# Adding the first four weighted V rows to the residual on VectorE, in a fused two-layer transformer kernel

## The chip, the cores and the metric

The kernel runs on one core of one Trainium2 chip. The metric is the device time of one execution in microseconds; lower is better. Engines are called TensorE (PE in the rows, with PEld for its weight loads), VectorE (DVE), ScalarE (ACT), GpSimd (POOL) and SyncE (SP, which only issues transfers here).

## The reference, cut to what matters

The kernel computes two whole layers on 256 tokens of width 1024 in float32. The part that the change touches is the second half of the first layer, a retrieval feed-forward: each token has 8 heads, each head picks 16 of 16,384 experts, and each expert is a row of U (for the dot product with the token) and a row of V (that is added with a weight).

```python
def peer_ffn(xn, w_q, sub_keys, u, v):
    q = (xb @ w_q).reshape(PEER_BLOCK, PEER_HEADS, 2, PEER_HALF)
    s = jnp.einsum('thpd,hpnd->thpn', q, sub_keys)      # scores of the sub-keys
    ...                                                  # top 16 of each head: expert, best
    g = jax.nn.softmax(best, axis=-1)
    act = jax.nn.gelu(jnp.einsum('td,thkd->thk', xb, u[expert]), approximate=False)
    return jnp.einsum('thk,thkd->td', (g * act).astype(xb.dtype), v[expert])
...
h = h + peer_ffn(hn, ...)
```

A token has 8 x 16 = 128 picks ("slots"). Tokens lie on the 128 partitions, in two tiles (n = 0 and 1), so the stage handles 2 x 128 = 256 "rows". Row k is, for every token of tile k // 128, the 2048 floats (U and V side by side) of its expert in slot k % 128: 1 MB gathered from memory.

## The kernel before, in words

The stages ahead of this one (first norm, projections, gated linear attention, output projection) end near 180 us of the trace, and the second layer begins near 860 us. Between them lies the retrieval stage. Its work, by engine:

- **SyncE** loads the eight pieces of the query weights (L684, each 1 MB, into five homes in turn), then waits for `v_done` of the batch that holds the first row in home `mixT` (row 6, so batch 3, L685), loads a 1 MB piece of the second layer's memory weights there (L687), and two more into query homes 0 and 1 (L690) once query groups 5 and 6 are done (L689).
- **TensorE** runs, for i = 0 to 7, `query_features(i)` (L1899: 16 float32 products of 128x256, which the trace shows as 32 passes), then `key_scores` of the group before (L2120). In i = 4, 5 and 6 it also runs two batches of `weighted_rows` (L2123 to L2131), so batches 0 to 5 stand between the query groups; the others follow in the loop at L2145. A batch is two rows. `weighted_rows(b)` waits for `diag_done`, and multiplies diag(weight of the row) by the V half of the row (two products of 128x512 per row, four passes in the trace, L2129), summed in two PSUM banks per tile of tokens over all 128 rows. It ends with `v_done` + 1.
- **VectorE** finds the picks of a head (`search_head`: some 40 small instructions, L1437 to L1502) and takes the dot product of the token with the U half of each row (`dot_rows`, L1548). It works in program order: search_head(0), search_head(1), rows 0 to 3, softmax(0), rows 4 to 7, search_head(2), rows 8 to 15, then head by head in the same pattern. At the end of a tile `add_peer` (L1516) adds the PSUM sums to `resid`.
- **ScalarE** copies query groups and key scores out of PSUM (`out_query`, L904; `out_scores`, L987) and runs `weigh(b)` for each batch: GELU of the dots (L1011, waits for `dot_done`), times the softmax weight (L1014, waits for `soft_done`), and the diagonal matrices (L1019), for which there are four buffers. In its order weigh(0) and weigh(1) follow out_scores(2); weigh(2) and weigh(3) follow out_scores(3); weigh(4) and weigh(5) follow out_query(5) and out_scores(4); weigh(6) and weigh(7) follow out_query(6) and out_scores(5). `out_scores(i)` waits for key_scores(i), which TensorE runs behind query_features(i + 1).
- **GpSimd** issues the gathers in order of rows (L805), each into a "home" of 8 KB per partition. A row in a home used before waits until the batch of the earlier row is summed (L800, `v_done`).

Homes near the change: rows 0 to 3 lie in early0 to early3, row 4 in ring5, 5 in query1, 6 in mixT, 7 in ring3 (free when query group 3 is done), 8 in ring4 (query group 4). Rows 9, 10, 11 and 12 reuse the homes of rows 0, 1, 2 and 3; rows 13, 14, 15 and 16 those of rows 4, 5, 7 and 8; rows 17, 18 and 19 those of 9, 10 and 11. Row 20 is the first in ring2, which is free when **query group 7**, the last one, is done (`home_ready`, L782). Row 21 (actT) waits for the same, rows 22 and 23 for the last key scores. As the issues are in order, no row behind row 20 can start before it.

```python
            for i in range(PH):
                query_features(i)
                ...
                elif i > 2:
                    key_scores(i - 1)
                if 4 <= i < PH - 1:
                    weighted_rows(2 * i - 8)
                    weighted_rows(2 * i - 7)
            key_scores(PH - 1)
            for b in range(2 * PH - 10, BATCHES):
                weighted_rows(b)
```

Of the kernel before, what the change touches and what calls it, by code (L numbers as in the profile page):

```python
# [9 lines left out]
ALU = mybir.AluOpType  # L10
# [4 lines left out]
D = 1024  # L15
# [18 lines left out]
PH = 8  # L34
HP = 2 * PH
NKEY = 128
TOP = 16
SLOTS = PH * TOP
# [2 lines left out]
PICKS = 2 * TOP  # L41
BATCH = 2
ROWS = NT * SLOTS
BATCH_ENDS = [*range(BATCH, ROWS - BATCH + 1, BATCH), ROWS - 1, ROWS]
BATCHES = len(BATCH_ENDS)
BATCHES_0 = SLOTS // BATCH
DIAGS = 2 * BATCH
# [39 lines left out]
def batch_of(k):  # L87

    return next(b for b, end in enumerate(BATCH_ENDS) if k < end)


def rows_of(b):

    return range(BATCH_ENDS[b - 1] if b else 0, BATCH_ENDS[b])

# [21 lines left out]
def build(nc, t, out):  # L117
    ctx = ExitStack()
    with ctx:
# [3 lines left out]
        def sem(name):  # L123
            return ctx.enter_context(nc.semaphore(name))
# [92 lines left out]
        mixT = take1(KC, T)  # L217
# [57 lines left out]
        soft_exp = sem("soft_exp")  # L275
        soft_done = sem("soft_done")
        dot_done = sem("dot_done")
        diag_done = sem("diag_done")
        v_done = sem("v_done")
        hq0a_then_mkv_moved = sem("hq0a_then_mkv_moved")  # L280
        peer_out = sem("peer_out")
# [135 lines left out]
        def row_count(k):  # L417

            return 16 * (rows_in[home_of[k]].index(k) + 1)

        def home_free(name):

            return batch_of(rows_in[name][-1]) + 1

        def unit_of(u):

# [222 lines left out]
        def _(sp):  # L649
# [28 lines left out]
            for i in range(PH):  # L678
# [3 lines left out]
                    sp.wait_ge(*query_used(i - WQ_HOMES))  # L682
                src = t["peer_w_q"][:, i * T:(i + 1) * T].rearrange("(c p) n -> p c n", p=P)
                sp.dma_start(wq_view(i), src).then_inc(wq_loaded[i % WQ_HOMES], 16)  # L684
            sp.wait_ge(v_done, batch_of(rows_in["mixT"][0]) + 1)  # L685
            sp.wait_ge(cols_then_mem_loaded, 80)
            sp.dma_start(mixT, w_mem[:, :, T:2 * T]).then_inc(cols_then_mem_loaded, 16)  # L687
            for k in range(2):
# [38 lines left out]
        def _(pool):  # L727
# [62 lines left out]

            for k in range(ROWS):
                n, s = k // SLOTS, k % SLOTS
                if k == PICKS * (UNITS - 2):
                    inverse_rms(0)
                if k % TOP == 0:
                    pool.wait_ge(idx_done, k // TOP + 1)
                name = home_of[k]
                earlier = [m for m in rows_in[name] if m < k]
                if earlier:
                    pool.wait_ge(v_done, batch_of(earlier[-1]) + 1)  # L800
                    if name == "mixT" and len(earlier) == 1:
                        pool.wait_ge(group_done, group_no["mk1"] + 1)
                elif name in home_ready:
                    pool.wait_ge(*home_ready[name])
                pool.indirect_dma_start(out=row_home[name], out_offset=None, in_=t["uv"],  # L805
                                        in_offset=bass.IndirectOffsetOnAxis(ap=idx[:, n, s:s + 1], axis=0)).then_inc(row_loaded[name], 16)
# [21 lines left out]
        def _(act):  # L828
            steps = [0]

            def link(ins):
                steps[0] += 1
                ins.then_inc(act_step, 1)
                act.wait_ge(act_step, steps[0])
# [170 lines left out]
            def weigh(b):  # L1005

                rows = rows_of(b)
                n, slots = rows[0] // SLOTS, range(rows[0] % SLOTS, rows[-1] % SLOTS + 1)
                now = slice(slots[0], slots[-1] + 1)
                act.wait_ge(dot_done, b + 1)  # L1010
                link(act.activation(gel[:, n, now], dots[:, n, now], ACT.Gelu))  # L1011
                act.wait_ge(soft_done, rows[0] // PICKS + 1)
                for s in slots:
                    ins = act.activation(wcol[:, n, s:s + 1], gel[:, n, s:s + 1], ACT.Copy, scale=gsoft[:, n, s:s + 1])  # L1014
                link(ins)
                if rows[-1] >= DIAGS:
                    act.wait_ge(v_done, batch_of(rows[-1] - DIAGS) + 1)
                for s in slots:
                    ins = act.activation(diag[:, s % DIAGS], ident[:], ACT.Copy, scale=wcol[:, n, s:s + 1])  # L1019
                ins.then_inc(diag_done, 1)  # L1020

            def squares(n):

# [230 lines left out]
        def _(dve):  # L1254
# [249 lines left out]
            def search_head(j):  # L1504
                search(j // PH, j % PH, 1, (j + 1) // 2 if j % 2 else 0)
# [9 lines left out]

            def add_peer(n):  # L1516

                dve.wait_ge(v_done, (BATCHES_0, BATCHES)[n])
                for half in range(2):
                    part = resid[:, n, half * TILE:(half + 1) * TILE]  # L1520
                    dve.tensor_tensor(part, part, ps[:, 4 + 2 * n + half, :], ALU.add).then_inc(peer_out, 1)
# [15 lines left out]
            def scale_rows(n):  # L1537

                dve.wait_ge(rstd_done, 6 + n)
                dve.tensor_scalar(scaled2[:, n], scaled2[:, n], rstd_x[:, n:n + 1], None, ALU.mult).then_inc(scaled_done, 1)  # L1540

            def dot_rows(first, last):

                for k in range(first, last):
# [5 lines left out]
                    if k + 1 in BATCH_ENDS:  # L1550
                        ins.then_inc(dot_done, 1)

            search_head(0)
            search_head(1)
            for j in range(NT * PH):
                first = TOP * j
                if j == PH:
                    dve.wait_ge(group_out, group_no["wq31"] + 1)
                    dve.tensor_tensor(hn_ps[1], scaled_p[:, 1], gain_row, ALU.mult).then_inc(gain_loaded_then_used, 1)
                    dve.wait_ge(gain_loaded_then_used, 17)  # L1560
                if j == NT * PH - 1:
                    scale_rows(0)
                dot_rows(first, first + 4)
                if j % 2 == 0:
                    softmax(j // 2)
                dot_rows(first + 4, first + 8)
                if j + 2 < NT * PH:
                    search_head(j + 2)
                if j == PH + 1:
                    add_peer(0)  # L1570
                    normed(0)
                if j == PH + 3:
                    mean_square(0)
                dot_rows(first + 8, first + TOP)
# [283 lines left out]
        def _(pe):  # L1858
# [263 lines left out]

            def weighted_rows(b):  # L2123

                pe.wait_ge(diag_done, b + 1)
                for k in rows_of(b):
                    n, s = k // SLOTS, k % SLOTS
                    for half in range(2):
                        ins = pe.matmul(ps[:, 4 + 2 * n + half, :], diag[:, s % DIAGS], row_home[home_of[k]][:, D + half * TILE:D + (half + 1) * TILE],  # L2129
                                        start=(s == 0), stop=(s == SLOTS - 1))  # L2130
                ins.then_inc(v_done, 1)  # L2131

            for i in range(PH):
                query_features(i)
                if i == 0:
                    pe.wait_ge(cols_then_mem_loaded, 80)
                if i < 2:
                    key_scores(i)
                elif i > 2:
                    key_scores(i - 1)  # L2140
                if 4 <= i < PH - 1:
                    weighted_rows(2 * i - 8)
                    weighted_rows(2 * i - 7)
            key_scores(PH - 1)
            for b in range(2 * PH - 10, BATCHES):  # L2145
                weighted_rows(b)
                if 8 <= b < 24:
                    memory(2 * b, 2 * b + 2)
# [366 lines left out]
```

## Time and profile before

| what | value |
|---|---|
| median of 3 runs | 1242.96 us (1242.66 to 1243.34) |
| the profiled execution's own time | 1242.78 us |
| its span, first to last instruction | 1241.0 us |
| TensorE busy | 1095.7 us, 88% |
| VectorE busy | 802.8 us, 65% |
| ScalarE busy | 493.3 us, 40% |
| GpSimd busy | 293.6 us, 24% |
| moved by the gathers (queue q0) | 268.45 MB |
| mean traffic over the span | 293 GB/s |

How to read it: the page of the profile divides the span into 40 slices of 31 us; a digit is the busy share in tenths, and the traffic in GB/s stands per slice. The retrieval stage covers slices 7 to 27 (186 us to some 854 us). The busy shares of the whole span mix stages that have different limits, so the rows below are from this stage. Times in the rows are microseconds from the start of the span; the profiled execution takes 1.8 us more than its span, and lies 0.2 us under the median.

### The profile page before, as it was taken

How to read it: one execution, taken by the hardware profiler on the slowest of the kernel's cores; microseconds unless marked ns; L12 is line 12 of the kernel's file. 1: busy time of each engine (PE TensorE's matmuls, PEld its weight loads, DVE VectorE, ACT ScalarE, POOL GpSimd, SP SyncE). 2: the span in 40 equal slices, each digit the busy share in tenths (PEclk: the TensorE clock that was granted, in tenths of full speed). 3: DMA queues.
4: the chain of work that ended last, by engine and by line, in shares of the span. 5: the costliest groups of instructions: out<-in, count | busy, mean ns of one | idle time of the engine just before them, and what ended most of it. 6: DMA issues, size and time to landing. Idle time of an engine off the chain costs nothing.

```text
span 1241.0 us, 13610 instructions
## 1 busy us (share of the span) xinstructions
PE 1095.7 (88%) x4932; PEld 740.0 (60%) x4932; DVE 802.8 (65%) x1713; ACT 493.3 (40%) x1046; POOL 293.6 (24%) x313
## 2 busy tenths in 40 slices
PE   9999999999977868788398676887999999999997
PEld 9888877654433323233143232334988988888886
DVE  6587546656776677756875677454776655756574
ACT  5657323224232332232242423223477343574433
POOL 1054103243354333434152533420001000000001
PEclk9999999999989988988699888899999999999999
DMA  5543269999999999999999999997344233443622
GB/s 210 203 171 136 86 204 357 361 421 421 421 422 421 421 421 422 420 422 421 409 421 422 421 421 421 421 422 296 136 170 144 109 126 140 160 172 137 237 78 110
DMA packets 61844, 364.01 MB, mean 293 GB/s; under 512 B 6848, under 2 KB 17360, under 8 KB 20304
## 3 DMA queue, kind: packets, MB, share of 16 engines
q0 software_dynamic: 36864, 268.45, 52.2%
q1 hardware_dynamic: 24448, 94.48, 21.4%
q8 instruction: 39, 0.64, 0.2%
q10 hardware_dynamic: 464, 0.20, 0.1%
q14 instruction: 29, 0.24, 0.1%
HBM read 361.01 MB, written 2.10 MB: 293 GB/s over the span
## 4 chain that ended last, share of the span: by engine, by line
PE 60%; DMA 21%; DVE 9%; issue 4%; ACT 2%; POOL 2%; DVEq 0%; POOLq 0%; ACTq 0%
PE ps L1966 19%; PE ps L2129 17%; DMA big<-in_uv,big 12%; PE ps L1932 10%; DMA ring<-in_uv,big 9%; PE ps L1899 4%; PE ps L2017 2%; DVE lo L1304 2%; DVE big L1548 1%; PE ps L1862 1%; POOL big L805 1%; ACT hi L883 1%; PE ps L2120 1%; POOL ring L805 1%; DVE ring L1548 1%
## 5 line engine op out<-in xcount | busy, mean ns | idle before, releaser
L2129 PE MATMUL ps<-big 128*128 128x512 f32 x540 | 268.0, 643 | 88.7 <-ACT big L1019 82.2
L2129 PEld LDWEIGHTS ps<-big 128*128 128x128 f32 x540 | 109.6, 207 | 236.7 <-issue 137.0
L1548 DVE CUSTOM_DVE_ANT_0 big<-big,ps 128x1024 f32<-128x1024 f32 x135 | 163.0, 1220 | 116.6 <-DMA big<-in_uv,big 113.5
L1966 PE MATMUL ps<-hi,x 128*128 128x512 f32 x704 | 225.2, 394 | 1.6 <-DVE lo L1304 1.4
L1304 DVE TENSOR_TENSOR lo<-raw,hi 128x2048 fp32r<-128x2048 f32 x60 | 140.5, 2344 | 72.3 <-ACT hi L883 72.0
L2129 PE MATMUL ps<-ring,big 128*128 128x512 f32 x356 | 167.9, 609 | 21.2 <-ACT big L1019 21.2
L805 POOL DMA_INDIRECT big<-in_uv,big x135 | 128.5, 952 | 232.9 <-PE ps L2129 165.5
L1548 DVE CUSTOM_DVE_ANT_0 ring<-ring,ps 128x1024 f32<-128x1024 f32 x89 | 107.6, 1220 | 74.9 <-DMA ring<-in_uv,big 74.9
L1966 PEld LDWEIGHTS ps<-hi,x 128*128 128x128 f32 x704 | 132.2, 188 | 30.3 <-issue 2.2
L1011 ACT ACTIVATE big<-big 128x2 f32<-128x2 f32 x129 | 25.9, 201 | 293.8 <-DVE big L1548 289.7
L883 ACT ACTIVATE hi<-raw 128x2048 fp32r<-128x2048 f32 x60 | 114.6, 1910 | 69.8 <-PE ps L1966 42.9
L1966 PE MATMUL ps<-lo,x 128*128 128x512 f32 x352 | 137.2, 390 | 0.0
L2129 PEld LDWEIGHTS ps<-ring,big 128*128 128x128 f32 x356 | 68.5, 196 | 111.5 <-issue 80.4
L1019 ACT ACTIVATE big<-ident,big 128x128 f32<-128x128 f32 x256 | 88.9, 394 | 67.1 <-PE ps L2129 63.1
L805 POOL DMA_INDIRECT ring<-in_uv,big x89 | 83.6, 940 | 126.6 <-PE ps L2129 95.9
L1932 PE MATMUL ps<-x,hi 128*128 128x256 f32 x544 | 99.3, 285 | 1.0 <-DVE lo L1304 0.8
L1932 PEld LDWEIGHTS ps<-x,hi 128*128 128x128 f32 x544 | 84.6, 192 | 1.7 <-DVE lo L1304 1.2
L1932 PE MATMUL ps<-x,lo 128*128 128x256 f32 x272 | 77.0, 283 | 0.0
L1014 ACT ACTIVATE big<-big 128x1 f32<-128x1 f32 x256 | 61.6, 287 | 38.0 <-DVE big L1513 33.9
L1966 PEld LDWEIGHTS ps<-lo,x 128*128 128x128 f32 x352 | 66.2, 188 | 12.8
L1899 PE MATMUL ps<-actT,ring 128*128 128x256 f32 x256 | 56.5, 380 | 1.2 <-ACT actT L852 1.2
L1899 PEld LDWEIGHTS ps<-actT,ring 128*128 128x128 f32 x256 | 48.4, 190 | 9.1 <-ACT actT L852 1.5
(371 smaller groups left out, 1357.9 us busy)
## 6 DMA issues: line engine op xcount, KB each, us to landing
raw<-in_pieces SPq DMA_DIRECT2D x61, 1024.0 KB, 4.8
ring<-in_peer_w_q SPq DMA_DIRECT2D x8, 1024.0 KB, 9.9
big<-in_up SPq DMA_DIRECT2D x4, 2048.0 KB, 8.6
big<-in_uv,big POOLq DMA_INDIRECT x135
ring<-in_w_mem_kv SPq DMA_DIRECT2D x2, 1024.0 KB
ring<-in_uv,big POOLq DMA_INDIRECT x89
resid<-in_x SPq DMA_DIRECT2D x2, 512.0 KB, 4.8
raw<-in_pieces SPq DMA_DIRECT2D x2, 512.0 KB, 9.1
```

Source lines behind the costliest of these rows:

```text
L805: pool.indirect_dma_start(out=row_home[name], out_offset=None, in_=t["uv"], in_offset=bass.IndirectOffsetOnAxis(ap=idx[:, n, s:s + 1], axi ...
L883: act.activation(part_of(hi2, name), raw_piece(name), ACT.Copy).then_inc(piece_hi, 1)
L1011: link(act.activation(gel[:, n, now], dots[:, n, now], ACT.Gelu))
L1014: ins = act.activation(wcol[:, n, s:s + 1], gel[:, n, s:s + 1], ACT.Copy, scale=gsoft[:, n, s:s + 1])
L1019: ins = act.activation(diag[:, s % DIAGS], ident[:], ACT.Copy, scale=wcol[:, n, s:s + 1])
L1304: dve.tensor_tensor(part_of(lo2, name), raw_piece(name), part_of(hi2, name).bitcast(F32), ALU.subtract).then_inc(piece_lo, 1)
L1548: ins = dve.tensor_tensor_reduce(out=row, in0=row, in1=hn_ps[n], scale=1.0, scalar=0.0, op0=ALU.mult, op1=ALU.add, accum_out=dots[:, n, s: ...
L1899: ins = pe.matmul(ps[:, gbank(g), a * T:(a + 1) * T], w[:, c, a * P:(a + 1) * P], actT[:, c, :], start=(c == 0), stop=(c == KC - 1))
L1932: ins = pe.matmul(o, a, b, start=(c == 0 and k == 0), stop=(c == chunks - 1 and k == 2))
L1966: ins = pe.matmul(o, a, b[:, c], start=(s == 0 and c == 0 and k == 0), stop=(s == 1 and c == HALF - 1 and k == 2))
L2017: ins = pe.matmul(ps[:, 4 + 2 * tau + PLACE[h] // 4, at:at + P // 2], k[rows, f, tok], later_half(q[rows, f, tok], m), start=True, stop=True)
L2129: ins = pe.matmul(ps[:, 4 + 2 * n + half, :], diag[:, s % DIAGS], row_home[home_of[k]][:, D + half * TILE:D + (half + 1) * TILE], start=(s ...
```

## The change

The first four rows leave TensorE. For the two batches of rows 0 to 3 (`PAIRS` = 2), `weigh` on ScalarE stops after the weights, without diagonals; VectorE's new `sum_pair(b)` adds V times weight to `resid[:, 0]` with one instruction per row, each waiting for the one before. The waits for batches 0 and 1 turn to the new semaphore `pair_summed`; the numbers of `v_done` shift by two. VectorE's order for the first head becomes: rows 0 and 1, softmax(0), rows 2 and 3, sum_pair(0), rows 4 and 5, sum_pair(1), rows 6 and 7, search_head(2), rows 8 to 15. On TensorE, the sum of tile 0 starts with row 4, and the six batches that stand between the query groups are now batches 2 to 7 where they were 0 to 5; the loop behind starts with batch 8.

```diff
--- before.py
+++ after.py
@@ -41,6 +41,8 @@
 PICKS = 2 * TOP
 BATCH = 2
 ROWS = NT * SLOTS
+VECTOR_ROWS = 4
+PAIRS = VECTOR_ROWS // 2
 BATCH_ENDS = [*range(BATCH, ROWS - BATCH + 1, BATCH), ROWS - 1, ROWS]
 BATCHES = len(BATCH_ENDS)
 BATCHES_0 = SLOTS // BATCH
@@ -275,7 +277,8 @@
         soft_exp = sem("soft_exp")
         soft_done = sem("soft_done")
         dot_done = sem("dot_done")
-        diag_done = sem("diag_done")
+        weighed_then_diag_done = sem("weighed_then_diag_done")
+        pair_summed = sem("pair_summed")
         v_done = sem("v_done")
         hq0a_then_mkv_moved = sem("hq0a_then_mkv_moved")
         peer_out = sem("peer_out")
@@ -418,9 +421,13 @@
 
             return 16 * (rows_in[home_of[k]].index(k) + 1)
 
+        def summed(b):
+
+            return (pair_summed, b + 1) if b < PAIRS else (v_done, b - PAIRS + 1)
+
         def home_free(name):
 
-            return batch_of(rows_in[name][-1]) + 1
+            return summed(batch_of(rows_in[name][-1]))[1]
 
         def unit_of(u):
 
@@ -682,7 +689,7 @@
                     sp.wait_ge(*query_used(i - WQ_HOMES))
                 src = t["peer_w_q"][:, i * T:(i + 1) * T].rearrange("(c p) n -> p c n", p=P)
                 sp.dma_start(wq_view(i), src).then_inc(wq_loaded[i % WQ_HOMES], 16)
-            sp.wait_ge(v_done, batch_of(rows_in["mixT"][0]) + 1)
+            sp.wait_ge(*summed(batch_of(rows_in["mixT"][0])))
             sp.wait_ge(cols_then_mem_loaded, 80)
             sp.dma_start(mixT, w_mem[:, :, T:2 * T]).then_inc(cols_then_mem_loaded, 16)
             for k in range(2):
@@ -797,7 +804,7 @@
                 name = home_of[k]
                 earlier = [m for m in rows_in[name] if m < k]
                 if earlier:
-                    pool.wait_ge(v_done, batch_of(earlier[-1]) + 1)
+                    pool.wait_ge(*summed(batch_of(earlier[-1])))
                     if name == "mixT" and len(earlier) == 1:
                         pool.wait_ge(group_done, group_no["mk1"] + 1)
                 elif name in home_ready:
@@ -1012,12 +1019,15 @@
                 act.wait_ge(soft_done, rows[0] // PICKS + 1)
                 for s in slots:
                     ins = act.activation(wcol[:, n, s:s + 1], gel[:, n, s:s + 1], ACT.Copy, scale=gsoft[:, n, s:s + 1])
+                if b < PAIRS:
+                    ins.then_inc(weighed_then_diag_done, 1)
+                    return
                 link(ins)
-                if rows[-1] >= DIAGS:
-                    act.wait_ge(v_done, batch_of(rows[-1] - DIAGS) + 1)
+                if rows[-1] - DIAGS >= VECTOR_ROWS:
+                    act.wait_ge(*summed(batch_of(rows[-1] - DIAGS)))
                 for s in slots:
                     ins = act.activation(diag[:, s % DIAGS], ident[:], ACT.Copy, scale=wcol[:, n, s:s + 1])
-                ins.then_inc(diag_done, 1)
+                ins.then_inc(weighed_then_diag_done, 1)
 
             def squares(n):
 
@@ -1515,7 +1525,9 @@
 
             def add_peer(n):
 
-                dve.wait_ge(v_done, (BATCHES_0, BATCHES)[n])
+                dve.wait_ge(v_done, (BATCHES_0, BATCHES)[n] - PAIRS)
+                if n == 0:
+                    dve.wait_ge(pair_summed, PAIRS)
                 for half in range(2):
                     part = resid[:, n, half * TILE:(half + 1) * TILE]
                     dve.tensor_tensor(part, part, ps[:, 4 + 2 * n + half, :], ALU.add).then_inc(peer_out, 1)
@@ -1549,6 +1561,20 @@
                                                    accum_out=dots[:, n, s:s + 1])
                     if k + 1 in BATCH_ENDS:
                         ins.then_inc(dot_done, 1)
+
+            def sum_pair(b):
+
+                dve.wait_ge(weighed_then_diag_done, b + 1)
+                for k in rows_of(b):
+                    if k % 2:
+                        wait_marked()
+                    elif b:
+                        dve.wait_ge(pair_summed, b)
+                    ins = dve.scalar_tensor_tensor(resid[:, 0], row_home[home_of[k]][:, D:2 * D], wcol[:, 0, k:k + 1], resid[:, 0], ALU.mult, ALU.add)
+                    if k % 2:
+                        ins.then_inc(pair_summed, 1)
+                    else:
+                        mark(ins)
 
             search_head(0)
             search_head(1)
@@ -1560,6 +1586,18 @@
                     dve.wait_ge(gain_loaded_then_used, 17)
                 if j == NT * PH - 1:
                     scale_rows(0)
+                if j == 0:
+                    dot_rows(0, 2)
+                    softmax(0)
+                    for b in range(1, PAIRS):
+                        dot_rows(2 * b, 2 * b + 2)
+                        sum_pair(b - 1)
+                    dot_rows(VECTOR_ROWS, VECTOR_ROWS + 2)
+                    sum_pair(PAIRS - 1)
+                    dot_rows(VECTOR_ROWS + 2, 8)
+                    search_head(2)
+                    dot_rows(8, TOP)
+                    continue
                 dot_rows(first, first + 4)
                 if j % 2 == 0:
                     softmax(j // 2)
@@ -2122,12 +2160,12 @@
 
             def weighted_rows(b):
 
-                pe.wait_ge(diag_done, b + 1)
+                pe.wait_ge(weighed_then_diag_done, b + 1)
                 for k in rows_of(b):
                     n, s = k // SLOTS, k % SLOTS
                     for half in range(2):
                         ins = pe.matmul(ps[:, 4 + 2 * n + half, :], diag[:, s % DIAGS], row_home[home_of[k]][:, D + half * TILE:D + (half + 1) * TILE],
-                                        start=(s == 0), stop=(s == SLOTS - 1))
+                                        start=(k in (VECTOR_ROWS, SLOTS)), stop=(s == SLOTS - 1))
                 ins.then_inc(v_done, 1)
 
             for i in range(PH):
@@ -2139,10 +2177,10 @@
                 elif i > 2:
                     key_scores(i - 1)
                 if 4 <= i < PH - 1:
-                    weighted_rows(2 * i - 8)
-                    weighted_rows(2 * i - 7)
+                    weighted_rows(PAIRS + 2 * i - 8)
+                    weighted_rows(PAIRS + 2 * i - 7)
             key_scores(PH - 1)
-            for b in range(2 * PH - 10, BATCHES):
+            for b in range(PAIRS + 2 * PH - 10, BATCHES):
                 weighted_rows(b)
                 if 8 <= b < 24:
                     memory(2 * b, 2 * b + 2)
```

## Rows read from the trace of the kernel before

**Rows 1.** The page: TensorE's busy time; traffic in 40 slices of the span.
```profile
PE 1095.7 (88%) x4932; PEld 740.0 (60%) x4932; DVE 802.8 (65%) x1713; ACT 493.3 (40%) x1046; POOL 293.6 (24%) x313
...
DMA  5543269999999999999999999997344233443622
GB/s 210 203 171 136 86 204 357 361 421 421 421 422 421 421 421 422 420 422 421 409 421 422 421 421 421 421 422 296 136 170 144 109 126 140 160 172 137 237 78 110
```

**Rows 2.** Chain of waits, 180 to 280 us: start, us, what, instructions.
```profile
211.05 6.87 PE ps L2129 x16
217.92 6.91 PE ps L1899 x32
...
239.49 0.89 PE ps L2120 x8
...
247.25 6.91 PE ps L1899 x32
```

**Rows 3.** Timeline of GpSimd (start, us, what, [idle before, releaser]): rows 9, 13, 20.
```profile
214.76 0.93 POOL L805 DMA_INDIRECT big<-in_uv,big  x1 [3.39 <-PE ps L2129]
...
229.42 0.94 POOL L805 DMA_INDIRECT ring<-in_uv,big  x1 [9.05 <-PE ps L2129]
...
254.43 0.94 POOL L805 DMA_INDIRECT ring<-in_uv,big  x1 [4.73 <-PE ps L1899]
```

**Rows 4.** Timeline of VectorE, dot products of rows 5, 7, 13, 15, 16, 20.
```profile
211.43 1.22 DVE L1548 CUSTOM_DVE_ANT_0 big<-big,ps 128x1024 f32<-128x1024 f32 x1 [1.68 <-DMA big<-in_uv,big]
...
217.25 1.22 DVE L1548 CUSTOM_DVE_ANT_0 ring<-ring,ps 128x1024 f32<-128x1024 f32 x1 [1.67 <-DMA ring<-in_uv,big]
...
235.08 1.22 DVE L1548 CUSTOM_DVE_ANT_0 ring<-ring,ps 128x1024 f32<-128x1024 f32 x1 [1.94 <-DMA ring<-in_uv,big]
...
241.84 1.22 DVE L1548 CUSTOM_DVE_ANT_0 ring<-ring,ps 128x1024 f32<-128x1024 f32 x1 [1.97 <-DMA ring<-in_uv,big]
251.90 1.22 DVE L1548 CUSTOM_DVE_ANT_0 ring<-ring,ps 128x1024 f32<-128x1024 f32 x1 [8.83 <-DMA ring<-in_uv,big]
...
261.84 1.22 DVE L1548 CUSTOM_DVE_ANT_0 ring<-ring,ps 128x1024 f32<-128x1024 f32 x1 [1.26 <-DMA ring<-in_uv,big]
```

**Rows 5.** Busy time in stretches of 1 us; last columns: granted clock, DMA share, GB/s.
```profile
228.00:229.00 1.00, 1.00 (x4) 0.39 (x3) 1.00 (x3) 0.00 (x0) 0.00 (x0) 1.00 0.43 164
229.00:230.00 1.00, 1.00 (x4) 0.52 (x3) 1.00 (x3) 0.21 (x2) 0.58 (x1) 1.00 0.08 33
230.00:231.00 1.00, 1.00 (x4) 0.42 (x3) 1.00 (x3) 0.97 (x4) 0.69 (x2) 1.00 0.00 0
231.00:232.00 1.00, 1.00 (x4) 0.39 (x3) 1.00 (x3) 0.20 (x1) 0.60 (x1) 1.00 1.04 172
```

**Rows 6.** Timeline of ScalarE: parts of weigh(2), weigh(3) and weigh(6).
```profile
212.70 0.20 ACT L1011 ACTIVATE big<-big 128x2 f32<-128x2 f32 x1 [1.01 <-DVE big L1548]
...
218.51 0.20 ACT L1011 ACTIVATE big<-big 128x2 f32<-128x2 f32 x1 [3.23 <-DVE big L1548]
...
219.26 0.69 ACT L1019 ACTIVATE big<-ident,big 128x128 f32<-128x128 f32 x2
...
241.14 0.48 ACT L1014 ACTIVATE big<-big 128x1 f32<-128x1 f32 x2
```

**Rows 7.** Timeline of SyncE's queue: the memory weights.
```profile
232.62 0.37 SPq L687 DMA_DIRECT2D big<-in_w_mem_kv  x1
233.03 6.86 SPq L690 DMA_DIRECT2D ring<-in_w_mem_kv  x2
```

**Rows 8.** Groups by form: count, busy us, mean ns of one.
```profile
L1591 DVE SCALAR_TENSOR_TENSOR resid<-resid,small,big 128x1024 f32<-128x1024 f32 x2 | 2.5, 1282 | 0.0
```

**Rows 9.** TensorE behind a wait: its timeline twice, and the stretch of 1 us behind the first.
```profile
283.51 3.44 PE L2129 MATMUL ps<-past_actT,big 128*128 128x512 f32 x4 [2.50 <-ACT big L1019]
...
708.03 1.98 PE L2129 MATMUL ps<-big 128*128 128x512 f32 x4 [2.94 <-ACT big L1019]
...
285.00:286.00 1.00, 1.00 (x2) 0.34 (x1) 1.00 (x3) 0.95 (x4) 0.00 (x0) 0.50 1.04 434
```

## The prediction

> **What bounds the kernel now.** I read the page first. TensorE is busiest over the whole span, at 1095.7 us of 1241.0, but the traffic says that this is not one regime: from the ninth slice (248 us) to the end of the retrieval stage every slice but one moves 420 to 422 GB/s, and nowhere else does it come near that [rows 1]. That is a flat ceiling. Inside it TensorE waits for diagonals, ScalarE for dot products, and VectorE for gathered rows; from row 16 to row 20 the dot products start 9.94 us apart for four rows, 2.49 us each, where one takes 1.22 us [rows 4]. 1.05 MB in 2.49 us is that same 421 GB/s. So from 248 us on the stage is bound by the gathers: 256 rows have to pass, and time is lost or won only where the DMA engines stand empty or where the stream of rows is held up.
>
> So the second view is traffic in short stretches at the start of the stage, where the page's slices are below the ceiling (357 and 361 GB/s). There is one hole: 164, 33, 0 and 172 GB/s in the four microseconds from 228 us [rows 5]. Against 421 that is 0.61 + 0.92 + 1.00 + 0.59, about 3.1 us. Its cause is in GpSimd's timeline: the gather of row 13 is issued at 229.42 after 9.05 us of idle time that `v_done` of batch 2 ended [rows 3]. Traffic is back 1.8 us after that issue [rows 5].
>
> The third view, the chain of waits, shows what TensorE does meanwhile: an unbroken order of 6.87 us of weighted rows (16 passes, two batches), 6.91 us of a query group and 0.89 us of key scores, three times over, 14.67 us a turn; no row of waiting lies between them, and the last query group runs from 247.25 to 254.16 us [rows 2]. Its end lets row 20 be issued, at 254.43 [rows 3]. That is not yet late: row 20 lies behind others in the queue and is ready for its dot product only at 261.84 [rows 4]. An empty queue would have brought it in some 4.7 us (1.8 until traffic, 2.49 of transfer, and 0.4 for the ramp at which the hole ends: 172 GB/s in its last microsecond [rows 5]). So row 20 has a slack of about 261.84 - 4.7 - 254.43 = 2.7 us, and no more.
>
> **The change, part by part.**
>
> *VectorE's sums.* The nearest row is the same instruction form on the same `resid`, 1282 ns [rows 8]: 2.6 us a pair. The arrivals of rows 5 and 7 show 1.7 us of idle time ahead of each dot product [rows 4]. sum_pair(0) runs after the dot of row 3 and ends before row 5 is there; sum_pair(1) follows the dot of row 5 (211.43 + 1.22) and ends near 215.3; the dot of row 6 then ends near 216.5, and row 7's begins at 217.25 as before [rows 4]. Cost 0, covered by the wait for gathers. At twice that duration (2.56 us), the bound from above, both pairs no longer fit and the dot of row 7 ends some 3.7 us later. Below, no duration gives a gain: row 7's arrival decides. softmax(0) moves ahead of row 2 and costs nothing for the same reason.
>
> *Homes come free earlier.* Batches 0 and 1 are released near 209.5 and 215.3; row 9, issued at 214.76 before [rows 3], can go right behind row 8, at some 211.7. Rows 9 to 12 gain up to 3 us, but the queue is not empty then, so this alone is worth nothing. Batch 2 is worth more: TensorE now sums it in the turn that begins at 211, so row 13, held until 229.42 before, goes near 217.8. The hole at 228 us is filled: -3.1 us.
>
> *TensorE's order.* This is the term that decides. Six batches still stand between the query groups, so nothing is taken off that stretch; but they are batches 2 to 7, and these are not ready. In the first turn TensorE is free for batch 2 at 211.05 [rows 2]. ScalarE has the dots of rows 4 and 5 at 212.70 [rows 6]; GELU and weights take 0.75 (218.51 to 219.26), the diagonals 0.69, so batch 2 starts near 214.2 and ends at 217.6. Batch 3 needs row 7, whose dot begins at 217.25; weigh(3) is at its diagonals at 219.26 and done at 219.95 [rows 6]. So batch 3 starts at 220.05, ends at 223.5, and query group 5 starts there and not at 217.92: 5.6 to 5.8 us late.
> In the next two turns the rows have landed, but ScalarE's own order holds the diagonals: weigh(4) stands behind out_scores(4), which needs the key scores that TensorE runs directly ahead of batch 4. The old turn at 239.49 shows the time of it: key scores start, weights start at 241.14, take 0.48, and the diagonals 0.69 [rows 2, 6], so they are ready 2.9 us after the key scores began, where these take 0.89. Wait: 2.0 to 2.2 us in each of two turns. The four diagonal buffers don't add one, since the batch two back is summed by then.
> Sum for query group 7: 5.75 + 2.2 + 2.2 = 10.15 us; it ends near 264.3, and row 20 is issued near 264.6 where it was 254.43.
>
> *What the transfers do then.* Before, behind the hole, three rows (13 to 15), three 1 MB weight pieces and row 16 were in by 251.90, 20.6 us after traffic returned near 231.3 [rows 4, 5, 7]; with 4 x 2.49 for rows, a piece takes some 3.5 us. After, from 228.5 without a hole: rows 13 to 15, two pieces, rows 16 to 19, and the third piece (issued when query group 6 is done, near 247.3) come to 7 x 2.49 + 3 x 3.5 = 28 us, so the queue is dry from 256.5. The traffic returns at 264.6 + 1.8 = 266.4. The old hole of 3.1 us is exchanged for one of 9.9 us. Counted the other way, row 20 is in at 264.6 + 4.7 = 269.3 where it was at 261.84, +7.5. The two give +6.8 and +7.5; I take +7.3, nearer to the second since it holds no piece sizes.
>
> *After that.* Rows 20 on follow 2.49 us apart, and the whole stage shifts. TensorE has four rows less to do (4 x 1.72 = 6.9 us), but behind row 20 it is waiting for diagonals anyhow: 0. SyncE's waits move (the first memory piece goes at 223.5, not at 232.62 [rows 7]) and only fill the queue.
>
> **Sum.** 1242.8 for the profiled execution + 7.3 = 1250.1; against the median, 0.2 us higher, 1250.3. I say 1250.2, slower by 0.6%. A measurement of this kernel tells some 0.2%, 2.5 us, from no change.
>
> **Rivals.**
> *1. TensorE also loses its clock.* Behind a wait of 2.50 us four passes took 3.44 us, twice 4 x 0.43, at a granted clock of 0.50 (the lower level, 1.2 GHz); behind one of 2.94 us they took 1.98, which only the full clock (2.4 GHz) allows [rows 9]. The new waits are 3.1, 2.4 and twice 2.2 us. A fall costs 1.7 us; that behind the first is hidden by the wait for batch 3; the other three would give +1.7 to +5.2, so 1252 to 1255.5. The Trainium skill speaks for it ("TensorE: Matmul & The Clock Gate", section on HAM oscillation): waits between bursts of matmuls send the engine back to the throttled state, and the price is paid burst by burst. By that rule the sum would be 1255; the trace agrees in one row and not in the other.
> *2. Faster.* If only the hole at 228 us counts, the gain is its 3.1 us: 1239.9. This is decided at row 20: it needs the last query group to be late by less than 2.7 us. My working has 10.2, and even with no wait at all in turns two and three 5.7 would remain, so little speaks for it; rows 9 to 19 being issued earlier does.
> *3. Nothing to be seen.* Later slack takes the delay up. One slice shows 409 GB/s where the others show 421, that is 0.9 us of loss in the stream [rows 1]; it can't take 7. It would need waits of half my size: 1241 to 1245.
> *4. Smaller waits.* If the ScalarE turns cost 1 us and batch 3 comes sooner: 1245.5 to 1248.
> *5. VectorE's instruction costs double:* +3.7, 1254.
>
> **How the numbers follow.** Forecast (1248 to 1252) 0.52; clock 0.25; VectorE 0.04; smaller waits 0.07; nothing 0.05; faster 0.07. The range of 8 in 10 leaves out rivals 2 and 3 and the ends of 1 and 4: 1246.5 to 1255. Chances: faster 0.07, same 0.05, slower 0.88.
>
> **What would show it.** In the changed profile: no idle time of GpSimd before row 13 to near 229; TensorE idle at 211 and 217.6 us for 3.1 and 2.4 us, released by the diagonals, and at some 231 and 248 for about 2.2; the last query group ending near 264; GpSimd idle for over 20 us before row 20 (242 to 264.6); traffic at zero from about 257 to 266 and none of it at 229; L1548 waiting up to 13 us for row 20; then 421 GB/s to the end. The prediction is wrong if query group 7 ends before 257 us, if the stream behind row 20 makes up the delay, or if a sum on VectorE takes much more than 1.28 us.

## The result and the profile after

The changed kernel takes 1254.93 us (median of 4 runs, 1252.95 to 1256.83), against 1243.15 for the kernel before: ratio 1.0091, interval 1.0079 to 1.0104. In a second comparison (e8 below) it was 1252.94 against 1244.24, ratio 1.0069 (1.0055 to 1.0083). It is slower by 9 to 12 us; 1250.2 was forecast, in a range up to 1255.

The page, with the lines that answer to [rows 1]:

```profile
span 1252.9 us, 13578 instructions
...
PE 1105.1 (88%) x4916; PEld 743.8 (59%) x4916; DVE 806.6 (64%) x1717; ACT 492.4 (39%) x1042; POOL 294.2 (23%) x313
...
DMA  5543269969999999999999999997344233443622
GB/s 208 201 169 134 85 202 363 411 239 423 420 422 421 422 421 421 421 421 421 422 405 422 421 421 421 421 422 308 136 172 161 102 135 135 145 180 145 234 74 113
```

Slice 8 rose from 361 to 411 GB/s: the hole at 228 us is gone. Slice 9 fell from 421 to 239: a longer one has come. The traffic in stretches of 3 us (last columns: granted clock, DMA share, GB/s) shows its edges:

```profile
254.00:257.00 3.00, 3.00 (x8) 1.33 (x7) 1.23 (x2) 0.00 (x0) 0.00 (x0) 1.00 0.61 230
257.00:260.00 3.00, 3.00 (x10) 1.71 (x9) 0.00 (x0) 0.00 (x0) 0.00 (x0) 1.00 0.00 1
260.00:263.00 3.00, 3.00 (x15) 2.66 (x14) 0.00 (x0) 0.00 (x0) 0.00 (x0) 1.00 0.00 0
263.00:266.00 3.00, 3.00 (x16) 2.64 (x16) 0.00 (x0) 0.00 (x0) 0.00 (x0) 1.00 0.00 0
266.00:269.00 3.00, 2.02 (x16) 1.66 (x15) 0.00 (x0) 1.36 (x3) 1.88 (x2) 1.00 0.35 74
269.00:272.00 3.00, 1.19 (x2) 0.68 (x3) 0.30 (x1) 2.87 (x11) 2.32 (x3) 0.83 1.01 404
```

GpSimd's timeline, first gather and rows 9, 13, 19 and 20, as in [rows 3]:

```profile
191.49 1.24 POOL L812 DMA_INDIRECT big<-in_uv,big  x1 [22.27 <-DVE big L1512]
...
213.35 0.94 POOL L812 DMA_INDIRECT big<-in_uv,big  x1 [0.30 <-issue]
...
221.34 0.94 POOL L812 DMA_INDIRECT ring<-in_uv,big  x1 [2.23 <-PE ps L2167]
...
243.65 0.94 POOL L812 DMA_INDIRECT big<-in_uv,big  x1 [0.30 <-issue]
266.27 0.94 POOL L812 DMA_INDIRECT ring<-in_uv,big  x1 [21.68 <-PE ps L1937]
```

Rows 9 and 13 no longer wait long, and row 20 waits 21.68 us for the products of the last query group. TensorE's timeline, first batch of each turn, and batch 3 in the second line (compare [rows 2], where no wait stands):

```profile
215.67 3.12 PE L2167 MATMUL ps<-ring,big 128*128 128x512 f32 x4 [2.94 <-ACT big L1029]
...
221.49 1.98 PE L2167 MATMUL ps<-big 128*128 128x512 f32 x4 [0.42 <-ACT big L1029]
...
235.00 1.99 PE L2167 MATMUL ps<-ring,big 128*128 128x512 f32 x4 [2.02 <-ACT big L1029]
...
251.95 1.98 PE L2167 MATMUL ps<-past_actT,big 128*128 128x512 f32 x4 [2.02 <-ACT big L1029]
```

ScalarE in the second turn: weigh(4)'s diagonals stand behind both copies.

```profile
232.13 0.60 ACT L911 ACTIVATE big<-ps 128x512 f32<-128x512 f32 x1 [10.70 <-PE ps L1937]
233.03 0.60 ACT L994 ACTIVATE big<-ps 128x512 f32<-128x512 f32 x1 [0.29 <-PE ps L2158]
...
234.26 0.69 ACT L1029 ACTIVATE big<-ident,big 128x128 f32<-128x128 f32 x2
```

VectorE: the second pair of sums, between the dot products of rows 5 and 7; then the dot products of rows 20 to 23 and the last of all:

```profile
212.91 1.22 DVE L1560 CUSTOM_DVE_ANT_0 big<-big,ps 128x1024 f32<-128x1024 f32 x1 [0.95 <-DMA big<-in_uv,big]
...
214.06 1.28 DVE L1573 SCALAR_TENSOR_TENSOR resid<-big,resid 128x1024 f32<-128x1024 f32 x1
215.37 1.28 DVE L1573 SCALAR_TENSOR_TENSOR resid<-past_actT,big,resid 128x1024 f32<-128x1024 f32 x1
...
218.73 1.22 DVE L1560 CUSTOM_DVE_ANT_0 ring<-ring,ps 128x1024 f32<-128x1024 f32 x1 [0.94 <-DMA ring<-in_uv,big]
...
271.70 1.22 DVE L1560 CUSTOM_DVE_ANT_0 ring<-ring,ps 128x1024 f32<-128x1024 f32 x1 [14.99 <-DMA ring<-in_uv,big]
275.56 1.22 DVE L1560 CUSTOM_DVE_ANT_0 actT<-actT,ps 128x1024 f32<-128x1024 f32 x1 [2.63 <-DMA actT<-in_uv,big]
278.27 1.22 DVE L1560 CUSTOM_DVE_ANT_0 big<-big,ps 128x1024 f32<-128x1024 f32 x1 [1.48 <-DMA big<-in_uv,big]
280.75 1.22 DVE L1560 CUSTOM_DVE_ANT_0 big<-big,ps 128x1024 f32<-128x1024 f32 x1 [1.25 <-DMA big<-in_uv,big]
...
869.94 1.22 DVE L1560 CUSTOM_DVE_ANT_0 big<-big,ps 128x1024 f32<-128x1024 f32 x1 [1.27 <-DMA big<-in_uv,big]
```

**Three stretches.** The first gather marks the end of everything that the change doesn't touch. It is issued at 191.49 us here and at 189.82 in the kernel before. From there to the start of the last dot product is "the stage" in what follows: 869.94 - 191.49 = 678.45 us, before 858.66 - 189.82 = 668.84. So of the 11.9 us between the spans, 9.6 lie in the stage, 1.7 ahead of it and 0.6 behind. The 1.7 are no part of the change (worked out at the end of the last section); the experiments are therefore compared by the stage as well as by time.

### The profile page after: what moved, and what is told of

It is laid out like the page before. It is cut to its first block, busy times and chain, and to the rows that moved or that the text cites. A ratio compares the mean times of both kernels' runs of the same rounds, so it can differ in the third digit from the quotient of the medians.

```text
span 1252.9 us, 13578 instructions
## 1 busy us (share of the span) xinstructions
PE 1105.1 (88%) x4916; PEld 743.8 (59%) x4916; DVE 806.6 (64%) x1717; ACT 492.4 (39%) x1042; POOL 294.2 (23%) x313
## 4 chain that ended last, share of the span: by engine, by line
PE 61%; DMA 21%; DVE 9%; issue 4%; POOL 2%; ACT 2%; DVEq 0%; POOLq 0%; ACTq 0%
PE ps L2004 19%; PE ps L2167 19%; PE ps L1970 10%; DMA big<-in_uv,big 9%; DMA ring<-in_uv,big 9%; PE ps L1937 3%; DMA past_actT<-in_uv,big 3%; PE ps L2055 2%; DVE lo L1314 1%; PE ps L2118 1%; DVE big L1560 1%; PE ps L1900 1%; POOL big L812 1%; ACT hi L890 1%; DVE ring L1560 1%
## 5 line engine op out<-in xcount | busy, mean ns | idle before, releaser
L2167 PE MATMUL ps<-ring,big 128*128 128x512 f32 x356 | 172.9, 624 | 24.1 <-ACT big L1029 24.1
```

## The experiments

Times are medians, each with its ratio to the kernel before on the same chip. "Lost" is what the traffic lacks of 421 GB/s, in microseconds, summed over 10 to 100 us behind the first gather in stretches of 2 us; "row 20" is its issue behind the first gather.

| kernel | time, us | ratio (interval) | stage, us | lost, us | row 20, us |
|---|---|---|---|---|---|
| before | 1243.15 to 1244.24 | | 668.8 | 4.8 | 64.6 |
| changed | 1254.93 | 1.0091 (1.0079 to 1.0104) | 678.5 | 14.6 | 74.8 |
| e1 one turn later | 1241.03 | 0.9974 (0.9965 to 0.9983) | 665.9 | 1.4 | 57.8 |
| e2 VectorE's work alone | 1243.03 | 1.0001 (0.9992 to 1.0010) | 668.7 | 4.8 | 64.6 |
| e3 weigh first | 1248.10 | 1.0036 (1.0024 to 1.0048) | 673.6 | 9.7 | 69.9 |
| e4 three, one, two | 1243.72 | 1.0001 (0.9992 to 1.0010) | 668.3 | 4.8 | 64.6 |
| e5 group 7 1.8 us late | 1245.48 | 1.0008 (0.9999 to 1.0017) | 669.8 | 6.2 | 66.4 |
| e6 group 7 10.3 us late | 1253.24 | 1.0077 (1.0063 to 1.0091) | 678.3 | 14.1 | 74.9 |
| e7 homes late | 1251.02 | 1.0054 (1.0039 to 1.0070) | 676.7 | 12.7 | 64.6 |
| e8 changed again | 1252.94 | 1.0069 (1.0055 to 1.0083) | 679.9 | 16.1 | 76.5 |
| e9 four, none, two | 1244.13 | 1.0002 (0.9992 to 1.0011) | 668.2 | 4.8 | 64.6 |
| e10 e1 again | 1240.77 | 0.9975 (0.9964 to 0.9985) | 665.9 | 1.5 | 57.7 |

e1 to e4, e5 to e8, and e9 with e10 were each measured together, beside the same runs of the kernel before. A "turn" is one round of TensorE's loop from i = 4 on: a query group, key scores and the batches behind them.

**e1.** The changed kernel, TensorE's batches moved:

```diff
-                if 4 <= i < PH - 1:
-                    weighted_rows(PAIRS + 2 * i - 8)
-                    weighted_rows(PAIRS + 2 * i - 7)
+                if 5 <= i < PH - 1:
+                    weighted_rows(PAIRS + 2 * i - 10)
+                    weighted_rows(PAIRS + 2 * i - 9)
...
-            for b in range(PAIRS + 2 * PH - 10, BATCHES):
+            for b in range(PAIRS + 2 * PH - 12, BATCHES):
```

> The changed kernel, but TensorE takes its first two batches (2 and 3) one turn later, after query group 5, batches 4 and 5 after group 6, and leaves the rest to the loop behind. My theory (TensorE's waits for diagonals hold back query group 7, and with it the gather of row 20): group 5 runs at once, batch 2 is ready by then, batch 3 with almost no wait, group 7 ends near 247 us where the kernel before has 254 and the changed one 266; row 20 is issued before the queue runs dry, there is no hole in the traffic at all, and the time is 3 us under the kernel before, some 1240. Rival 1 (VectorE's sums are what costs): the sums are all still there, so it stays near 1254. Rival 2 (the clock): group 7 is early, yet half-clock stretches keep the time above 1247.

Measured: 1241.03 us, 0.26% under the kernel before; as expected. The page shows 407 and 419 GB/s in slices 8 and 9. GpSimd waits at row 20 for the same 4.73 us as in the kernel before, where the changed kernel has 21.68:

```profile
GB/s 210 197 177 136 86 204 341 407 419 422 420 416 422 423 420 421 421 420 422 413 421 422 422 421 421 421 422 280 137 170 148 108 123 144 159 170 136 237 79 109
```

```profile
243.10 0.94 POOL L812 DMA_INDIRECT big<-in_uv,big  x1 [0.30 <-issue]
248.77 0.94 POOL L812 DMA_INDIRECT ring<-in_uv,big  x1 [4.73 <-PE ps L1937]
```

All four sums are still on VectorE, so they are not the cost; where TensorE's batches stand is. Row 20 goes 6.9 us earlier than before (64.6 to 57.8), just the four rows' 4 x 1.72 us. This is the version that beats both. It was run a second time as e10: 1240.77, again 665.9 us of stage.

> The changed kernel with TensorE's batches one turn later, once more, beside the version without VectorE's sums. My theory: 665.9 us from first gather to last dot product as before, 0.2 to 0.3% under the kernel before; it keeps 7 us of slack at row 20 where the version without sums has about none, so it is the faster of the two by up to 1 us. Rival: the two are the same.

**e2.** VectorE's part alone; its sums add the gain row times zero, and TensorE keeps rows 0 to 3:

```diff
+                if j == 0:
+                    dot_rows(0, 2)
+                    softmax(0)
+                    dot_rows(2, 4)
+                    add_nothing()
+                    dot_rows(4, 6)
+                    add_nothing()
+                    dot_rows(6, 8)
+                    search_head(2)
+                    dot_rows(8, TOP)
+                    continue
...
+                for _ in range(2):
+                    link(dve.scalar_tensor_tensor(resid[:, 0], gain_row, 0.0, resid[:, 0], ALU.mult, ALU.add))
```

> The kernel before, with VectorE's work of the change alone: softmax(0) after row 1 and four sums of the same form on resid, two after row 3 and two after row 5, that add the gain row times zero. TensorE, the homes and the order of the batches are those of before. My theory: no change, within 0.2% of the kernel before (1241 to 1245), the dot product of row 7 still beginning where its gather lands. Rival 1 (the sums cost): 3 us or more slower.

Measured: ratio 1.0001, stage 668.7. The cover named in the prediction holds; VectorE (columns as in [rows 4]):

```profile
210.54 1.22 DVE L1548 CUSTOM_DVE_ANT_0 big<-big,ps 128x1024 f32<-128x1024 f32 x1 [0.94 <-DMA big<-in_uv,big]
211.69 2.48 DVE L1556 SCALAR_TENSOR_TENSOR resid<-big,resid 128x1024 f32<-128x1024 f32 x2
...
216.36 1.22 DVE L1548 CUSTOM_DVE_ANT_0 ring<-ring,ps 128x1024 f32<-128x1024 f32 x1 [0.94 <-DMA ring<-in_uv,big]
```

Row 7's dot product still waits 0.94 us for its gather. The rival is out. These sums do not wait for ScalarE's weights as the real ones do; in the changed kernel's rows above no idle time stands before the sums either.

**e3.** The changed kernel, ScalarE's order in turns two and three:

```diff
             for i in range(PH):
+                if i in (5, 6):
+                    weigh(2 * i - 6)
                 out_query(i)
...
-                        weigh(2 * i - 6)
+                        if i < 5:
+                            weigh(2 * i - 6)
                         weigh(2 * i - 5)
```

> The changed kernel, with weigh(4) and weigh(6) on ScalarE ahead of the copy of the query group and of the scores, so that the diagonals are ready when TensorE has run its key scores. This takes away the second and third new wait (2.0 us each by the changed kernel's trace) and leaves the first. My theory: group 7 ends 4 us earlier, near 262, and the time falls by the same 4 us, to some 1251, since the queue is dry from 256 us on. Rival (the stream of rows is held by something else, the time of row 20 does not decide): the time stays at 1254 to 1255.

Measured: 1248.10; stage 4.9 us shorter than the changed kernel's, row 20 issued 4.9 us earlier. TensorE has no wait left in these turns:

```profile
231.56 1.05 PE L2161 MATMUL ps<-big 128*128 128x128 f32 x8
232.45 1.89 PE L2170 MATMUL ps<-ring,big 128*128 128x512 f32 x4
...
246.23 1.05 PE L2161 MATMUL ps<-big 128*128 128x128 f32 x8
247.12 1.88 PE L2170 MATMUL ps<-past_actT,big 128*128 128x512 f32 x4
```

So about half of the loss in the stage was made by the order on ScalarE, in two waits printed as 2.02 us and worth 2.3 each at GpSimd (the rest of the 4.9 is 0.4 from the first turn); row 20 is still 5.2 us later than before, which is the first turn's wait. Each microsecond of row 20 was paid in full: 4.9 were taken off it where 4 had been expected, and 4.9 off the stage.

**e4.** The kernel before, six batches as 3, 1, 2:

```diff
-                if 4 <= i < PH - 1:
-                    weighted_rows(2 * i - 8)
-                    weighted_rows(2 * i - 7)
+                for b in {4: (0, 1, 2), 5: (3,), 6: (4, 5)}.get(i, ()):
+                    weighted_rows(b)
```

> The kernel before, with the six batches between the query groups parted as 3, 1 and 2 and not 2, 2 and 2; all on TensorE, nothing on VectorE. Group 7 ends where it did (254 us) and row 13 is issued near 221 us, not at 229.4. My theory (only holes in the gather traffic cost time): the hole of 3.1 us at 228 us is gone and the time is 3 us less, 1240. Rival (the hole is hidden by later waits, or another one takes its place): 1243, no change.

Measured: ratio 1.0001: a miss, and the rival is right. Stretches of 3 us:

```profile
233.00:236.00 3.00, 3.00 (x14) 2.29 (x13) 2.04 (x4) 1.17 (x4) 0.94 (x1) 1.00 0.67 213
243.00:246.00 3.00, 3.00 (x8) 1.33 (x7) 0.78 (x2) 0.85 (x4) 0.20 (x1) 1.00 1.03 350
246.00:249.00 3.00, 3.00 (x10) 1.59 (x9) 0.00 (x0) 0.89 (x4) 1.95 (x3) 1.00 0.70 201
```

The hole moved behind row 14, since row 15 and the memory weights wait for batch 3, and a second one came ahead of row 16.

**e9.** The same in 4, 0, 2: `{4: (0, 1, 2, 3), 6: (4, 5)}`.

> The kernel before, all rows on TensorE and nothing on VectorE, with the six batches parted as 4, 0 and 2. Group 7 ends where it did (254 us), row 13 is issued near 221.4 and row 15 near 224.7 us. My theory (only holes in the gather traffic cost, and the changed kernel's gain at 228 us can be had without VectorE): no hole at 228 nor at 234, the queue just reaches row 20; 2 to 3 us less than the kernel before, first gather to last dot product 666 to 667 us, time 1241 to 1242. Rival (as in the parting 3, 1, 2, the hole only moves): 668.5 us, no change.

Measured: ratio 1.0002, a miss again. 406 GB/s from 228 us on, but the hole stands ahead of row 16, which waits for batch 4:

```profile
228.00:231.00 3.00, 3.00 (x15) 2.65 (x14) 3.00 (x7) 0.00 (x0) 0.00 (x0) 1.00 1.01 406
243.00:246.00 3.00, 3.00 (x8) 1.33 (x7) 0.00 (x0) 1.28 (x5) 1.18 (x2) 1.00 0.42 160
```

Both expectations had left out where the later rows' homes come from. None of the partings tried closes the hole with all rows on TensorE, which is busy without a break there; taking four rows off it (e1) does. Nor could they have won 3 us: in each of them row 20 still goes at 64.6 us, since query group 7 ends where it did, and by the measured price of an empty queue (worked out under "the term that was mis-sized" below) that leaves, as an estimate, 0.6 to 0.9 us to win; e4 and e9 have 0.6. e10, measured beside e9, is 3.4 us faster than it, where at most 1 had been expected. So VectorE's sums were worth 3 us, once TensorE was not made to wait.

**e5, e6.** The kernel before, TensorE held up right ahead of group 7, by 8 and by 46 idle products:

```diff
                 bank_free(g)
+                if i == PH - 1:
+                    keep_busy(gbank(g), 46)
```

> The kernel before, with 8 idle products of 128x128 on TensorE right ahead of the products of query group 7, in the PSUM bank that the group then overwrites: group 7 and row 20 some 1.8 us later, nothing else changed. My theory: row 20 has a slack of 2.7 us in the queue, so the time is that of the kernel before, within 0.2% (the stretch from first gather to last dot product 668.8 us, as before). Rival (every delay of group 7 is paid in full): 1.8 us more, 670.6.

> The same with 46 idle products: some 10.2 us late, the delay of group 7 that I reckoned for the change, with all else as in the kernel before, so without VectorE's sums and without any wait for diagonals. My theory: row 20 is issued as late as in the changed kernel, and the stage grows by the same 9.6 us (668.8 to some 678.4 us from first gather to last dot product), time near 1253. Rival 1 (the delay less the slack, 7.5 us, is all that the late row costs, and the rest comes from elsewhere in the change): 676.3 us. Rival 2 (the sums or the moved batches cost): under 3 us.

Measured: e5 issues row 20 1.8 us late and its stage is 0.9 us longer; the ratio's interval just includes 1. Neither the theory (0) nor the rival (1.8) is met: 0.9 us of the delay went unpaid. The slack of 2.7 us was not there: the dot product of row 20 starts 1.7 us later behind the first gather (73.7 against 72.0), that of row 23 1.3 us later. e6 has row 20 at 264.70, 10.3 us late, and its stage is 678.3 us, that of the changed kernel within 0.2:

```profile
248.76 0.94 POOL L805 DMA_INDIRECT big<-in_uv,big  x1 [0.30 <-issue]
264.70 0.94 POOL L805 DMA_INDIRECT ring<-in_uv,big  x1 [15.00 <-PE ps L1901]
```

With no sum on VectorE and no wait for a diagonal, a late last query group alone makes the whole loss, as expected. And e6 still has the hole at 228 us, which the changed kernel has filled: in the changed kernel the filled hole won nothing, the queue ran dry that much sooner.

**e7.** The kernel before in 0, 2, 4: `{5: (0, 1), 6: (2, 3, 4, 5)}`.

> The kernel before, all rows on TensorE, with its six batches parted as none, 2 and 4 over the three turns: group 7 ends where it did (254 us), but row 9 can be issued only near 222.4 us and row 13 near 237.1. My theory (holes in the gather traffic are what costs, whatever makes them): one hole near 219 to 224 us of some 5.7 us and one near 234 to 239 of some 4.7 us in place of the one of 3.1 us, so 7.3 us slower, 1251; with slow restarts behind each hole up to 1253. Rival (only the end of query group 7 matters): 1243, no change.

Measured: 1251.02, as expected. Row 20 goes at 64.6 us as before, yet the stage is 7.8 us longer. Rows 9 and 13 are what is late:

```profile
223.62 0.93 POOL L805 DMA_INDIRECT big<-in_uv,big  x1 [11.19 <-PE ps L2129]
...
238.28 0.93 POOL L805 DMA_INDIRECT ring<-in_uv,big  x1 [8.96 <-PE ps L2129]
```

So it is no property of group 7: a hole elsewhere costs as well. The table says the same in general: from before to changed, e1, e3, e5, e6, e7 and e8 the lost time moves by +9.8, -3.4, +5.0, +1.4, +9.3, +8.0 and +11.4 us, and the stage by +9.6, -3.0, +4.7, +0.9, +9.5, +7.8 and +11.1.

**e8.** The changed kernel again.

> The changed kernel once more, for its spread. My theory: the stretch from first gather to last dot product takes 678.4 us again, within 0.5 us, while the stretch ahead of the first gather differs from run to run by 1 to 2 us with the clock of TensorE in it (189.8 us before and 191.5 in the changed kernel's profile, though no instruction of it was touched). Rival (the change made the stretch ahead slower): 191.5 us again, in all runs of it.

Measured: 1252.94. The stage is 679.9 us, not 678.4 within 0.5: a miss. The first gather is issued at 191.09 us, which alone decides nothing on the part ahead of it. Row 20 comes 1.7 us later than in the first profile, all of it from the second turn, and the stretches show why (first e8's, then the changed kernel's first profile; the third column from the right is the granted clock):

```profile
216.00:219.00 3.00, 3.00 (x5) 1.35 (x4) 2.07 (x4) 0.00 (x0) 1.87 (x2) 0.50 1.02 412
235.00:238.00 3.00, 3.00 (x6) 1.31 (x5) 1.33 (x3) 0.90 (x4) 0.00 (x0) 0.68 1.01 406
```

```profile
216.00:219.00 3.00, 3.00 (x5) 1.19 (x4) 2.06 (x4) 0.00 (x0) 1.92 (x3) 0.56 1.02 412
235.00:238.00 3.00, 3.00 (x7) 1.44 (x8) 1.23 (x2) 1.22 (x5) 0.00 (x0) 1.00 1.02 411
```

After the same wait of 2.0 us TensorE's clock fell in one execution and not in the other.

## Why the prediction was right, point by point

- **What bounds the stage** (gathers at 421 GB/s, only holes cost): right, shown by e6, e7 and the columns of stage and lost time.
- **VectorE's sums cost nothing**: right; 1.28 us each, and e2 shows the cover.
- **The hole at 228 us is filled**: right, slice 8. It was priced at 3.1 us; e1, without any hole, gained 3.0. In the changed kernel itself it was worth nothing, as e6 shows.
- **TensorE's waits**: forecast 3.1, 2.4, 2.2 and 2.2 us; measured 2.94, 0.42, 2.02 and 2.02. Behind the first the clock fell (0.56 over 216 to 219 us), batch 2 took 5.4 us instead of 3.6, and that filled the wait for batch 3, as rival 1 said it would. The sum was right: row 20 was forecast at 264.6 - 189.8 = 74.8 us behind the first gather and came at 266.27 - 191.49 = 74.8.
- **The term that was mis-sized: the price of the empty queue.** The prediction had "an empty queue would have brought it in some 4.7 us", a slack of 2.7 us, and so +7.5 by its second count, which goes by row 20 (it took +7.3 between its two counts). Row 20 took 271.70 - 266.27 = 5.4 us, 0.7 more, and the three rows behind it came 3.86, 2.71 and 2.48 us apart where 2.49 is the pace, 1.6 more. 7.5 + 0.7 + 1.6 is 9.8; the kernel before loses 0.2 in the same three rows, and 9.6 is what the stage grew by. From the issue of row 20 to the dot product of row 23 that is 14.5 us, and 14.2 to 14.4 in e3, e6 and e8, which also ran dry; the prediction's terms give 4.7 + 3 x 2.49 = 12.2. The kernel before, whose queue is not dry, takes 269.50 - 254.43 = 15.1 us there (row 23):

```profile
269.50 1.22 DVE L1548 CUSTOM_DVE_ANT_0 big<-big,ps 128x1024 f32<-128x1024 f32 x1 [1.10 <-DMA big<-in_uv,big]
```

  So the slack was 0.6 to 0.9 us and not 2.7, which agrees with e5 (0.9 unpaid) and e6 (10.3 late, 9.5 paid). The first count (+6.8) was short as well: the lost time in the table grew by 9.8 us. Its 3.5 us for a memory piece is an estimate that no run tried.
- **Rival 1 (the clock)** came beside the forecast and not in its place: hidden at the first wait, and in e8 also at the second, +1.5 us of stage. The Trainium skill ("TensorE: Matmul & The Clock Gate", HAM oscillation) tells this of waits for transfers that are longer than these, so it promised no fall here; the rows show one behind one or two of the four new waits and none behind others of the same length.
- **Rival 2 (faster)** was said to need group 7 less than 2.7 us late. By the measured slack a version with the hole filled gains at most 0.6 to 0.9 us with group 7 where it was (an estimate from the rows above), and for the whole 3 us it must end earlier. e1 is the change in which it does, by 6.9 us.
- **Size and luck.** Direction and mechanism are no luck: e1, e3 and e6 show them. That the first measurement, 1254.93, still lies in the range up to 1255 is in part luck. It is 4.7 us above the forecast; 2.3 of these are the empty queue, and another 2.3 of the 11.9 us between the two spans lie outside the stage (1.7 ahead of the first gather, 0.6 behind the last dot product), where the prediction had put nothing.

## What to carry to other kernels

Work taken off an engine gives nothing if the freed place is filled with work whose inputs aren't ready: after such a change, compare each step's new place with the time at which its input is made, and with what stands ahead of that input in the other engine's order. Where transfers are the bound, count for every buffer when it is freed and look for holes in the traffic; closing one by reordering a fully busy engine moved it to the next buffer in both attempts here. A buffer that comes free at the same late time as before also caps the gain from closing holes ahead of it. And price a hole by its length plus the restart, not by its length alone.

## What had not been expected of the hardware

- **A restarted stream of gathers is slow for its first rows.** Behind a dry stretch of 11 us the first 1 MB row took 5.4 us from its issue, and the next two came 3.86 and 2.71 us later, against 2.49 in the stream. In e3, e6 and e8, dry at the same place, the first row took 5.6 to 5.7 us, the next 3.4 to 3.5, and the one behind it 2.5 to 3.0. That two rows share the engines at first would explain it; no run tried that.
- **TensorE's clock may or may not fall behind the same short wait**: it did behind 2.0 us in e8's second turn (0.68 over 3 us), not in the first profile (1.00), from the same program.
- **The same work ahead of the first gather takes 189.1 to 191.8 us** in twelve profiles: 191.49 and 191.09 in the changed kernel, 189.81 in e6 and 191.77 in e5, which differ only in a count far behind it. The granted clock between 50 and 60 us parts the twelve: it was 1.00 in the four with 189.1 to 189.8 us (before, e2, e6, e9) and 0.83 in the eight with 190.9 to 191.8, here the changed kernel's:

```profile
50.00:60.00 10.00, 9.10 (x46) 7.46 (x45) 4.59 (x2) 8.98 (x10) 0.00 (x0) 0.83 0.60 224
```

  The eight are the five profiles with the change (changed, e1, e3, e8, e10) and three without it (e4, e5, e7), so the profiles alone leave open whether the change makes the fall more likely. The medians say that it adds nothing there: e1 and e10 lie 2.9 and 3.1 us under the kernel before, and their stages account for 3.0. So two or three microseconds of a single profile's span say nothing on a change of this kernel; the stage, measured between two instructions, repeats within 0.2 us where the clock holds (e1 and e10: 665.9 both).
